# A recurrence on Trainium2: 32x32 blocks moved by DMAs from SyncE's queue in place of GpSimd's copies

## The reference

```
u = h @ w_in                              # 256 x 10240
q, a_f, a_b, i, z = jnp.split(u, 5, axis=-1)
log_f = jnp.logaddexp(jnp.log(lb), jnp.log1p(-lb) + jax.nn.log_sigmoid(a))
key   = (1.0 - lb) * jax.nn.sigmoid(-a)   # for a_f (forward) and a_b (backward)
```

## Time and profile before

| | us |
|---|---|
| median of 3 runs | 1892.46 |
| lowest and highest | 1892.26, 1892.69 |
| the profiled execution | 1893.24 |
| its span | 1891.4 |
| TensorE busy | 1886.1 |
| VectorE busy | 1301.9 |
| ScalarE busy | 1068.8 |
| GpSimd busy | 654.1 |

### The profile page before, as it was taken

One profiled execution on the slowest core, in us unless ns is written; L12 is line 12 of the kernel. 1 busy time (PEld: TensorE's weight loads), 2 busy tenths in 40 slices (PEclk: granted clock), 3 DMA queues, 4 the chain that ended last, 5 costly groups with the idle time before them and its releaser, 6 DMA issues.

```text
span 1891.4 us, 28799 instructions
## 1 busy us (share of the span) xinstructions
PE 1886.1 (100%) x10832; PEld 1556.8 (82%) x10832; DVE 1301.9 (69%) x1881; ACT 1068.8 (57%) x1414; POOL 654.1 (35%) x701
## 2 busy tenths in 40 slices
PE   9999999999999999999999999999999999999999
PEld 8888878888888888888888888888888888888887
DVE  5899987646888888887668877655555555544443
ACT  7444466546878787974555755544444444443332
POOL 1899832516051423302418646422222222210000
PEclk9999999999999999999999999999999999999999
DMA  9666555666555565555565455666666666655564
GB/s 326 193 190 189 178 175 192 192 196 180 168 174 172 154 182 168 169 166 179 189 192 153 151 175 177 209 193 192 187 198 194 194 192 195 191 195 193 192 195 159
DMA packets 183600, 352.64 MB, mean 186 GB/s; under 512 B 11840, under 2 KB 12352, under 8 KB 183488
## 3 DMA queue, kind: packets, MB, share of 16 engines
q1 hardware_dynamic: 183344, 351.12, 60.7%
q10 hardware_dynamic: 144, 0.01, 0.0%
HBM read 348.99 MB, written 2.10 MB: 186 GB/s over the span
## 4 chain that ended last, share of the span: by engine, by line
PE 96%; DVE 1%; POOL 1%; ACT 1%; POOLq 0%; DMA 0%; issue 0%; DVEq 0%; ACTq 0%; SPq 0%
PE acc L645 31%; PE acc L647 30%; PE acc L646 30%; PE T L760 1%; PE T L596 1%; POOL apad L507 1%; DVE w_lo L1295 1%; PE T L861 0%; PE acc L612 0%; PE T L770 0%; PE T L772 0%; PE T L751 0%; PE T L840 0%; POOLq L508 0%; DMA raw<-in_conv_w_in_dram 0%
## 5 line engine op out<-in xcount | busy, mean ns | idle before, releaser
L1295 DVE TENSOR_TENSOR w_lo<-raw,w_hi 128x1024 fp32r<-128x1024 f32 x564 | 698.5, 1242 | 508.4 <-ACT w_hi L907 498.7
L907 ACT ACTIVATE w_hi<-raw 128x1024 fp32r<-128x1024 f32 x655 | 686.9, 1057 | 593.4 <-PE acc L647 571.3
L645 PE MATMUL acc<-w_hi,h_hi 128*128 128x512 f32 x1872 | 734.6, 392 | 0.3 <-DVE w_lo L1295 0.3
L647 PE MATMUL acc<-w_hi,h_lo 128*128 128x512 f32 x1872 | 728.7, 389 | 0.0
L646 PE MATMUL acc<-w_lo,h_hi 128*128 128x512 f32 x1872 | 728.6, 389 | 0.0
L645 PEld LDWEIGHTS acc<-w_hi,h_hi 128*128 128x128 f32 x1872 | 351.4, 188 | 77.6 <-issue 3.8
L647 PEld LDWEIGHTS acc<-w_hi,h_lo 128*128 128x128 f32 x1872 | 351.4, 188 | 73.5
L646 PEld LDWEIGHTS acc<-w_lo,h_hi 128*128 128x128 f32 x1872 | 351.6, 188 | 71.4
L585 POOL COPY fT<-fq 32x256 f32<-32x256 f32 x176 | 111.7, 634 | 360.3 <-DVE fq L1786 353.4
L494 POOL TENSOR_TENSOR w_lo<-raw,w_hi 128x1024 fp32r<-128x1024 f32 x76 | 180.9, 2409 | 64.1 <-ACT w_hi L907 64.0
L1386 DVE SCALAR_TENSOR_TENSOR T<-vpad,feat,T 128x256 f32<-128x256 f32 x464 | 182.4, 478 | 0.0
(11 more groups left out here) (259 smaller groups left out, 1618.4 us busy)
## 6 DMA issues: line engine op xcount, KB each, us to landing
raw<-in_hgrn_w_in_dram SPq DMA_DIRECT2D x160, 512.0 KB, 3.7
raw<-in_conv_w_in_dram SPq DMA_DIRECT2D x96, 512.0 KB, 4.2
raw<-in_ffn_w_gate_dram SPq DMA_DIRECT2D x88, 512.0 KB, 4.4
raw<-in_ffn_w_up_dram SPq DMA_DIRECT2D x88, 512.0 KB, 3.7
raw<-in_ffn_w_down_dram SPq DMA_DIRECT2D x88, 512.0 KB, 4.4
raw<-in_attn_w_qkv_dram SPq DMA_DIRECT2D x40, 512.0 KB, 3.9
raw<-in_conv_w_out_dram SPq DMA_DIRECT2D x32, 512.0 KB, 4.3
raw<-in_hgrn_w_out_dram SPq DMA_DIRECT2D x32, 512.0 KB, 4.4
```

What stands on the lines that cost most here:

```text
L645: nc.tensor.matmul(o, hi[:, kt, a], w_hi[:, slot, kk, :], start=c == 0 and kk == 0, stop=False)
L647: last = nc.tensor.matmul(o, lo[:, kt, a], w_hi[:, slot, kk, :], start=False, stop=c == p.chunks - 1 and kk == CK - 1)
L907: A(w_hi[:, slot, :, :], raw[:, slot, :, :], ACT.Copy).then_inc(hi_ready, 1)
L1295: TT(w_lo[:, slot, :, :], raw[:, slot, :, :], rounded(w_hi[:, slot, :, :]), ALU.subtract).then_inc(split_ready, 1)
```

## The change

The 48 copies of a group leave GpSimd, which keeps `o_power`. SyncE begins 48 DMAs in their place, from SBUF to SBUF. A DMA takes 32 partitions of a source tile (quarter `a`) and eight runs of 32 elements (128 bytes) in each, and puts them on the 32 partitions of quarter `b`: 256 runs, 32 KB. They stand in the hooks of the next group's stream at ticks 1 to 12, four ahead of each of the twelve loads: `kf` at 1 to 4, `kb` at 5 to 8, `qT` at 9 to 12. SyncE waits for `g_q` ahead of each four. Each destination has a semaphore of its own, which 16 DMAs raise by 256; the readers wait for these in place of `g_M`. So that each run is whole, VectorE's transposes write four pieces of 128 elements with a stride in place of one row of 512.

```diff
+        def by_block(t):
+            return t.rearrange("p a b -> p (a b)").rearrange("p (k t i) -> p k t i", k=HPG, t=TB)
+
+        def rows_of(t, a, b):
+            return t.rearrange("p a b -> p (a b)")[a * QUARTER:(a + 1) * QUARTER, :].rearrange("p (c b i) -> p c b i", c=HPG * TB, b=4)[:, :, b, :]
+        gate_quarters = (sz, aftok, abtok)
...
+            def gate_moves(j, i, a):
+
+                sp.wait_ge(g_q, 3 * j + i + 1)
+                for b in range(4):
+                    sp.dma_start(rows_of((kf, kb, qT)[i], b, a), rows_of(gate_quarters[i], a, b)).then_inc(g_moved[i], 16)
+
+            def moves_of(j):
+                at = Hooks()
+                for i in range(3):
+                    for a in range(4):
+                        at.put(4 * i + a + 1, lambda i=i, a=a: gate_moves(j, i, a))
+                return at
             for j in range(4):
-                stream("hgrn", j, lambda k: (t["hgrn_w_in"][0], (1, 2, 0, 3)[k] * D + j * GC))
-            stream("hgrn_z", 0, lambda k: (t["hgrn_w_in"][0], 4 * D + k * GC))
+                stream("hgrn", j, lambda k: (t["hgrn_w_in"][0], (1, 2, 0, 3)[k] * D + j * GC), moves_of(j - 1) if j else None)
+            stream("hgrn_z", 0, lambda k: (t["hgrn_w_in"][0], 4 * D + k * GC), moves_of(3))
...
             for j in range(4):
-                pool.wait_ge(g_q, 3 * j + 1)
-                moves(kf, sz, range(4)).then_inc(g_M, 1)
-                pool.wait_ge(g_q, 3 * j + 2)
-                moves(kb, aftok, range(2))
-                if j:
-                    o_power(j - 1)
-                moves(kb, aftok, range(2, 4)).then_inc(g_M, 1)
-                pool.wait_ge(g_q, 3 * j + 3)
-                moves(qT, abtok, range(4)).then_inc(g_M, 1)
-            o_power(3)
+                o_power(j)
...
                 if s == 0:
-                    pe.wait_ge(g_M, 3 * j + 3)
+                    pe.wait_ge(g_moved[2], 256 * (j + 1))
...
-                act.wait_ge(g_M, 3 * j + 1 + d)
+                act.wait_ge(g_moved[d], 256 * (j + 1))
...
                 for tb in range(TB):
-                    V.transpose(dst[:, tb, :], src[:, tb, :])
+                    V.transpose(by_block(dst[:, :, :])[:, :, tb, :], src[:, tb, :].rearrange("p (k i) -> p k i", k=HPG))
```

More of the change, by code:

```diff
@@ L313, in build @@
             sem(f"ln_{s}") for s in ("z", "zT", "zc", "mean", "d", "sq", "var", "std", "n", "act", "g", "hi", "lo"))
-        g_raw, g_q, g_M, g_act, g_lb, g_D, g_E, g_G, g_mm, g_S = (
-            sem(f"hgrn_{s}") for s in ("raw", "quarters", "moved", "act", "lb", "D", "E", "G", "mm", "S"))
+        g_raw, g_q, g_act, g_lb, g_D, g_E, g_G, g_mm, g_S = (
+            sem(f"hgrn_{s}") for s in ("raw", "quarters", "act", "lb", "D", "E", "G", "mm", "S"))
         g_sb, g_K = sem("hgrn_blocks"), sem("hgrn_keys")
+        g_moved = [sem("hgrn_moved_kf"), sem("hgrn_moved_kb"), sem("hgrn_moved_q")]
         g_av, g_o, g_ss, g_std, g_on, g_zr, g_z, g_y, g_yT, g_hi, g_lo = (
@@ L518, in o_power @@
                 nc.gpsimd.drain()
[L520 to L524, removed]
-            for j in range(4):
-                pool.wait_ge(g_q, 3 * j + 1)
-                moves(kf, sz, range(4)).then_inc(g_M, 1)
-                pool.wait_ge(g_q, 3 * j + 2)
-                moves(kb, aftok, range(2))
-                if j:
-                    o_power(j - 1)
-                moves(kb, aftok, range(2, 4)).then_inc(g_M, 1)
-                pool.wait_ge(g_q, 3 * j + 3)
-                moves(qT, abtok, range(4)).then_inc(g_M, 1)
-            o_power(3)
+            for j in range(4):
+                o_power(j)
             x_moves(2)
@@ L1063, in raw_out @@
                     if k < 2:
-                        act.wait_ge(g_M, 3 * (j - 1) + k + 2)
+                        act.wait_ge(g_moved[k + 1], 256 * j)
                     elif k == 3:
@@ L1173, in hz_out @@
             def hz_out(k):
-                act.wait_ge(g_M, 12)
+                act.wait_ge(g_moved[1], 1024)
+                act.wait_ge(g_moved[2], 1024)
                 evacuate("hgrn_z", 0, k, 1, gate_rows[k], ACT.Silu if k == 3 else ACT.Copy, g_zr)
@@ L1540, in weigh @@
                 if s == 1:
-                    dve.wait_ge(g_M, 3 * j + 3)
+                    dve.wait_ge(g_moved[2], 256 * (j + 1))
                 TT(e[:, 1, :, :], e[:, 1, :, :], qT[:, :, :], ALU.mult).then_inc(g_G, 1)
@@ L1589, in quarters @@
                 if i == 0 and not is_first(j):
-                    dve.wait_ge(g_M, 3 * j - 2)
+                    dve.wait_ge(g_moved[0], 256 * j)
                 for tb in range(TB):
-                    V.transpose(dst[:, tb, :], src[:, tb, :])
+                    V.transpose(by_block(dst[:, :, :])[:, :, tb, :], src[:, tb, :].rearrange("p (k i) -> p k i", k=HPG))
                 settle().then_inc(g_q, 1)
```

## The result

The changed kernel takes 1897.22 us (median of 8 runs, 1895.52 to 1900.28), the kernel before 1892.46 us beside it (8 runs, 1892.02 to 1893.03). The ratio is 1.0027, with a 95% interval of 1.0018 to 1.0036: slower, by 4.8 us between the medians. The runs of the changed kernel also scatter over 4.8 us where those of before scatter over 1.0. The profiled execution is the fastest of the eight, 1895.52 us, 2.3 us over the profiled execution of before (1893.24). So the traces show half of the loss; of the rest, 1.7 us lie between this execution and the median of its kernel, and 0.8 us between the other and its own.

The account below looks back on a forecast made before the run. TensorE, busy 1886.1 of 1891.4 us, was taken to bound the kernel. `kf` 1.3 us late less 1.0 shorter gave 0.3 us a group, + 1.2 over four: 1892.46 + 1.2 = 1893.7 us, range 1890.5 to 1913.

Parts of the forecast that it names:

- rival A: DMA engines: 128-byte packets cost more, x from 0.45 us, blocks late at tick 7 or `level`; 1896.9, likeliest 1900; chance 0.27.
- The floor: TensorE, busy 1886.1 of 1891.4 us, bounds the kernel; only 5.3 us idle, so changes elsewhere win little.
- Rival C: Faster: `kf` in time and 1.0 us less on the chain; four groups give 1 us, 1891.5; chance 0.04.
- What the moves cost SyncE: SyncE's queue: 0.51 us a move, 0.41 a load, 2.45 us a tick against 3.2, so room.
- Rival B: A queue fills up, in the engines or SyncE (1.0 us a move): much slower, 1950 to 2180; chance 0.17.
- The step's threshold: SyncE's room within the 3.2 us tick would be used up at 0.70 us a move.
- `qT` "0.8 us to spare": At `level`: tick 11's load 0.3 us later, `qT` there at 679.1 against a shifted 679.9, 0.8 us to spare.
- The DMA engines' part: 16 DMA engines: 19 ns a packet, 0.3 us a move, 2.5 us a tick, under 3.2.
- `kf` late: At ScalarE's `gates`: `kf` lands at 653.05 against 651.71, 1.3 us late a group, 0.7 at the least.
- The relief on VectorE: Without GpSimd's copies, four splits and three steps of line 1477 on the chain to tick 7 shorten by 1.0 us.
- `kb` "just hidden": At ScalarE's step wanting `kb`: moves land at 666.8, wanted at 665.68, shifted to 667.0, so just hidden.
- The transposes with a stride: VectorE at ticks 28, 30 and 31: taken as costing nothing, up to 1.3 us more for `kf` in the range.

Follow-up runs that it names:

- the whole-tensor run: Changed kernel with each tensor moved in one DMA of 128 partitions of 4 KB, three a group, blocks left in old places: 1891.99 us, 0.9996 of the kernel before.
- the two kernels below it: Changed kernel, 48 DMAs a group kept, each of 32 pieces of 1 KB (1892.99 us) or of 128 partitions of 256 bytes (1892.74 us).
- the run of 24 DMAs: Changed kernel with 24 DMAs a group of 64 partitions, 512 packets of 128 bytes each, in place of 48: 1892.05 us, 0.9997 of the kernel before.
- the run with the tiny DMAs: Changed kernel plus a DMA of 32 partitions x 4 bytes behind each four moves, 12 a group: 1929.87 us, 1.0193 of the kernel before.

## Why the prediction's range held and its likeliest case did not come

The time lies in the range of 1890.5 to 1913, but the likeliest case, no change that can be told, did not come: forecast + 1.2 us, measured + 4.8. The range held by rival A's part of it, and rival A's mechanism is not what happened, so that is luck.

- **The floor: right.** TensorE bounds the kernel and nothing off it can win. Rival C's condition, blocks in time and VectorE relieved, was met by the whole-tensor run, and gave 0.9996.
- **What the moves cost SyncE: this step failed.** "I take 0.51 us for a move, and 0.41 us for a load. Four moves and a load make 2.45 us a tick". They make 0.65 and 0.65 with the gaps, 3.25 us. The 0.47 us of the earlier trace rows is no DMA that came alone: it was begun at 61.01, 0.04 us behind a load. At its start the kernel before even has nine DMAs from HBM in a row without a pause, with holds of 0.39 to 0.55 us and 0.67 for the last; four of them, from SyncE's timeline of before:

```profile
3.15 0.55 SPq L423 DMA_DIRECT2D raw<-in_conv_w_in_dram  x1
3.74 0.48 SPq L400 DMA_DIRECT2D szt<-in_x_turned_dram  x1
4.26 0.45 SPq L423 DMA_DIRECT2D raw<-in_conv_w_in_dram  x1
4.75 0.67 SPq L400 DMA_DIRECT2D szt<-in_x_turned_dram  x1
```

  So standing in a row does not make the price by itself. What no row of before shows is a DMA behind a move from SBUF to SBUF, and that is where a move and a load alike hold SyncE for about 0.6 us, a load behind `qT`'s one whole DMA too (0.59). Why stays open. Rival B's "no issue in the trace much above 0.47 us" was a misreading as well: there are 0.67, 0.79 and 1.20 us. The step's threshold failed too. It took the 3.2 us between loads, pauses included, as the time that SyncE has. With all holds at 0.65 the same sum gives (3.2 - 0.65) / 4 = 0.64 us a move; but the two kernels below it, at 3.08 and 3.09 us a tick, hardly pause either. What decides is the last move against `level`.
- **`qT` "0.8 us to spare": fell with it.** It took tick 11's load as 0.3 us late. It was 2.2 us later, 1.3 of it beyond the shift of 0.9, and TensorE waited 0.75 us in that group, 2.7 us in four. The 4.9 us from that load to the last landing were right: 676.12 to 681.06. Each us of lateness did go to TensorE in full, as the prediction says.
- **The DMA engines' part: right.** x = 0.3 us for a move came from 19 ns a packet. From 660 to 684 us the changed kernel moved 9689 packets, 7641 of them small, with the engines 85.5% busy: 0.855 x 16 x 24 = 328 us, less 2048 x 80 ns = 164 us, leaves 21 ns for each small one, at the most. With 85.5% the engines were nearer to full than the 78% of the forecast (2.5 of 3.2 us), but the run with the same packets in half the issues lost nothing. Rival A named the right size (1896.9 and more) and the right sign, idle TensorE ahead of `level`, with the wrong place: not the packets fall behind but the queue that begins them. Rival B named the place, the queue, but at 1.0 us a hold.
- **`kf` late: right in kind, more in size.** 2.1 us a group, forecast 1.3. Its moves landed after 2.6 us, sooner than forecast, but the last began 2.7 us later (652.8 against 650.1), 0.9 of it the shift. The load ahead of the last four adds 0.24 us and each of three moves 0.14; one of these moves held SyncE for 1.34 us, 0.7 more than the others; and the load itself began 0.35 us late.
- **The relief on VectorE: right in kind, but its size was more than twice the forecast.** Forecast 1.0 us, from the splits and the steps of line 1477. The scan and line 1474 gained too, which I had not looked at. The rows of the two kernels (ns least/median/most), which answer to the earlier trace rows:

```profile
L1474 DVE TENSOR_SCALAR E<-kf,lbj x16: 481/516/518, 469.3 to 769.4; 128x256 f32<-128x256 f32 x16
```

```profile
L1485 DVE TENSOR_TENSOR_SCAN Bc<-Bc x16: 811/814/880, 465.1 to 766.1; 128x256 f32<-128x256 f32 x16
```

```profile
L1301 DVE TENSOR_TENSOR w_lo<-raw,w_hi x14: 1195/1221/1227, 634.9 to 675.9; 128x1024 fp32r<-128x1024 f32 x14
...
L1480 DVE TENSOR_SCALAR E<-kf,lbj x16: 344/348/357, 470.4 to 771.5; 128x256 f32<-128x256 f32 x16
...
L1483 DVE SCALAR_TENSOR_TENSOR E<-kb,lbj,E x16: 476/478/487, 471.6 to 773.1; 128x256 f32<-128x256 f32 x16
...
L1491 DVE TENSOR_TENSOR_SCAN Bc<-Bc x16: 660/665/683, 466.9 to 769.0; 128x256 f32<-128x256 f32 x16
```

  The first two rows are of before. Splits 4 x 0.15, scans 4 x 0.15, line 1474 (now 1480) 4 x 0.17 at the medians, line 1477 (now 1483) 3 x 0.13: together 2.3 us. The group of j=2 shows it as a whole: `gates` begins 3.0 us later than before (654.70 against 651.71), tick 7 on TensorE 0.8 (674.71 against 673.90), so 2.2 us were won on the way. That is why the doubled lateness of `kf` cost nothing: two terms of the sum were both too small, and that they cancel is luck. The Trainium skill, "SBUF — State Buffer", "Who interferes with whom", has VectorE's instructions with two inputs in SBUF contend with GpSimd's reads, and lets a `tensor_scalar` contend in its fast modes. The trace agrees for the split and the scan, 1371 to 1221 and 814 to 665 ns. Line 1474's `tensor_scalar` gained most, 516 to 348 ns; whether it runs in such a mode no row tells.
- **`kb` "just hidden": wrong by a little.** 1.6 us in three groups, on ScalarE. It did not reach TensorE: tick 7 came no later than the shift.
- **The transposes with a stride: right.** They cost nothing: 684 to 687 ns for 512 columns in either kernel.

What stays open is the scatter, and with it 1.7 us between the median and the profiled execution. In the profile six moves held SyncE for over 0.75 us, and each overlaps a packet of 16 KB from a queue that the profile calls "instruction". The DMA view from 649.7 to 651.5 us, where a move of `kf` held it 1.34 us (queue: packets, MB, share of the 16 engines):

```profile
q1 hardware_dynamic: 726, 0.17, 65.9%
q8 instruction: 1, 0.02, 4.2%
```

But in the run of 24 DMAs five moves hold SyncE for 0.88 to 1.32 us with no such packet near, so this can't be the whole cause. Where the last move is late anyway, a long hold ahead of it makes it later, and that fits a scatter of 4.8 us. The two kernels at 3.08 and 3.09 us a tick had holds of up to 2.3 and 1.7 us and scatter over only 1.7 and 1.6 us: their last moves have 1 us more of room. A rival is the clock: two of the three slowest of the changed kernel's eight runs (1898.91 and 1900.28 us) have a mean granted clock of 0.999, the six others 1.000, and 0.001 of the span is 1.9 us. Neither was tested, and no trace of a slower run exists.

## What to carry to other kernels

An issuing engine is a resource of its own: sum up its holds from its first issue to the last that somebody waits for, add the landing, and compare this with the moment at which the reader is ready. Take the hold from a row that stands behind the same kind of DMA, and for the transfers queued among them too: a load held SyncE for 0.37 us alone and for 0.6 behind a move. A queue without pauses costs nothing as long as its last issue is in time, as at 3.08 us a tick; at 3.24 it was 0.4 to 0.9 us late in each group, and each further DMA ahead of it, of whatever size, costs about its full hold. When moves must be many, fewer and wider ones are worth more than smaller ones. It also helped to take a third of them off the queue that the weights use.

## What the runs showed of the hardware

- A DMA that stands right behind one from SBUF to SBUF holds SyncE for 0.58 to 0.64 us at the median, whether it moves 128 bytes in 32 packets, 32 KB in 32, 128 or 256, 64 KB in 512, or is a load of 512 KB. The same load alone holds it 0.37 us, and 0.43 to 0.55 in a row of DMAs from HBM. The first move behind a load lies at 0.48 us (128 partitions), 0.51 (32 packets), 0.59 (256) and 0.60 (512). The Trainium skill, "DMA: Bandwidth & Descriptors", "Issuing engines are not separate DMA queues", says that beginning a DMA usually takes little beside the DMA itself. Here it takes 0.65 us beside a landing of 2.9, and since landings overlap and issues don't, the issues decided.
- A packet of 128 bytes between two places in SBUF takes 21 ns of an engine at the most, about a quarter of the 80 ns of a 2 KB packet. The price of small runs lay below what I had feared.
- GpSimd's copies slow VectorE's split by 12% (1221 to 1371 ns), the scan by 22% (665 to 814) and the `tensor_scalar` of line 1474 by 48% (348 to 516).
- A wait can cost TensorE more than its own length. In the run with the tiny DMAs the granted clock fell from 1.00 to 0.50 seven times, each time around the end of a wait of 2.3 to 3.3 us, and 4.5 us of the loss stood behind the waits at `level`.
- DMAs that GpSimd begins hold it for 0.58 us each. They bought nothing beside SyncE's: `kb`'s moves landed 1.2 us later.
